# Two-block transformer kernel on one core: the passages between the expert blocks are reordered, and the dilated values' product is computed inside the block of queries and keys

## Chip, core and metric

The kernel runs on one core of one Trainium2 chip. Engines are named as in the profile: PE (TensorE matmul) and PEld (its weight loads), DVE (VectorE), ACT (ScalarE), POOL (GpSimd), SP (SyncE, here an issuer of DMAs). Times are device microseconds of one execution; the metric is the median of the runs.

## What is computed

Two transformer layers over 512 tokens of width 1024, all in float32. Both end in a PEER layer of experts, and these two hold most of the time:

```python
def peer_ffn(h, w_query, sub_keys, expert_u, expert_v):
    ...
        q = (xc @ w_query).reshape(PEER_CHUNK, PEER_HEADS, 2, PEER_HALF)
        s1 = jnp.einsum('thc,hnc->thn', q[:, :, 0], sub_keys[:, 0]).astype(jnp.float32)
        s2 = jnp.einsum('thc,hnc->thn', q[:, :, 1], sub_keys[:, 1]).astype(jnp.float32)
        v1, i1 = lax.top_k(s1, PEER_TOPK)
        v2, i2 = lax.top_k(s2, PEER_TOPK)
        cand = (v1[..., :, None] + v2[..., None, :]).reshape(PEER_CHUNK, PEER_HEADS, PEER_TOPK * PEER_TOPK)
        top, ci = lax.top_k(cand, PEER_TOPK)
        ...
        gate = jax.nn.softmax(top, axis=-1)
        act = jax.nn.gelu(jnp.einsum('td,thkd->thk', xc, u).astype(jnp.float32), approximate=False)
        wts = (gate * act).astype(xc.dtype)
        return jnp.einsum('thk,thkd->td', wts, vv)
```

There are 16384 experts of width 1024, 8 heads, and 16 experts chosen per head. The second layer also has an attention over strided keys (dilated), whose queries, keys and values are columns of one projection:

```python
    qa, ka, va, qb, kb, vb, gl = jnp.split(proj, IN_SPLITS, axis=-1)
    qa = rope(rms_norm(qa.reshape(b, s, DIL_HEADS, HEAD_DIM), qn_a), positions)
    ka = rope(rms_norm(ka.reshape(b, s, DIL_HEADS, HEAD_DIM), kn_a), positions)
    va = va.reshape(b, s, DIL_HEADS, HEAD_DIM)
```

## The kernel before

The program is a row of blocks. In a block every engine has its own list of instructions and they meet only by semaphores; at its end all engines wait for each other (in the trace: POOLq and PEq L83), so what one engine has left over at the end holds up all. Each float32 product is made of three passes of rounded halves: ACT rounds an operand (`hi`, a CAST), DVE subtracts (`lo`, TENSOR_TENSOR), and PE multiplies hi*hi, lo*hi and hi*lo. `rehearse` is ten small matmuls with no result of use at the start of some blocks.

**The expert layers** (`peer`, tags p1 and p2). For 384 of the 512 tokens every expert is computed densely, expert tile by expert tile: 128 tiles of 128 experts. For the first 128 tokens the chosen rows are gathered one by one (`Fetched`): POOL issues an indirect DMA per row into a ring of four, and DVE takes it (L1334 a dot product, L1342 an addition). Three blocks share the dense work:

- `peer_choose` (L1490). PE makes the scores of four token tiles of 128 tokens, DVE picks the best from them, and meanwhile the first 56 expert tiles (`TT * EARLY`, 14 per token tile) are multiplied by `A.multiply` (L1439, 24 matmuls into one of two banks). ACT empties a bank by `A.gelu` (L1421), then rounds the tile four further on (`split_hi`, L1410; four slabs) and stores the result (L1398). DVE's `split_lo` (L1429) stands between its steps of choosing, at places written out by hand. SP loads the tiles (L1389), four ahead. After the seventh tile of each token tile ACT waits for DVE's `shifted` and makes the exponential (L1568). `turn` (L1530) transposes the chosen indices and gates of a token tile, ACT copies them to `rows` (L1557).
- `peer_gates` (L1747 and on). PE multiplies the other 72 expert tiles and, behind each, one or two of 96 *steps*: a step is four tokens, whose one-hot rows `hot1` (times the gate) and `hot2` DVE makes (L1760, L1762) and whose remainder ACT makes (L1797), multiplied at L1787 into a ring of four. ACT copies the product to `kept` (L1815). Twelve *pieces* of eight steps each arise so; `kept` has room for two, so SP stores ten of them to `gates` in HBM (L1824), 2 MB each, and ACT waits for the store of piece n-2 before it writes piece n. SP's store of a piece stands two loads after its end. At the block's start ACT rounds all gates at once and DVE makes the relative rest of them (`rest_of_gates`, L1739 to L1745).
- `peer_values` (L1931): 128 tiles again, gates times activations times values.

**The second layer's projection.** `queries_keys` (L2996) multiplies nine chunks of 512 columns, seven of queries and keys and two of values (of the other attention); each has eight slabs, five of which are held split. Then `product` with tag va multiplies the dilated values, a chunk of 256 columns and one of 512, in a block of its own with its own split of the same input `hT`; `dilated_attention` (tag dat) follows.

## Time and profile before

| | us |
|---|---|
| median of three runs (3761.3 to 3764.9) | 3764.0 |
| the profiled execution, its own time | 3765.4 |
| its span, first to last instruction | 3763.2 |
| PE busy in it | 3601.9 |
| DVE busy | 2971.0 |
| ACT busy | 1724.5 |
| mean granted clock of PE, as a share of 2.4 GHz | 0.981 |

Where the first expert layer lies in the span: its choosing block from 667 to 926 us, the gates block to 1320, the values block to 1846; queries and keys run from 1870 to 2081, the dilated values to 2120; the second expert layer repeats the first one's blocks from 2573 on. The profile gives each instruction's start and length. Matmuls overlap: the next one starts before the one before is over, so distances from start to start count, and the number in square brackets behind a row is the time for which the engine idled before it, with what ended that. A clock below 1 (PEclk) is the share of full speed that PE was granted.

### The profile page before, as it was taken

The page shows a single profiled execution, that of the slowest core. Times are in us where ns is not written, and L with a number is a line of the kernel's source. Part 1 is how long each engine was busy: PE and PEld are TensorE (multiplying, and loading weights), DVE is VectorE, ACT ScalarE, POOL GpSimd, SP SyncE. Part 2 cuts the span into 40 slices and gives each one's busy share as a digit, 9 for nine tenths or more (in the row PEclk, how much of TensorE's full clock was granted, in tenths as well). Part 3 has the DMA queues.
Part 4 walks back from the last instruction along what each step waited for, and adds up shares of the span by engine and source line. Part 5 has one row for each costly group of instructions (what it writes and reads, how often), then busy time and mean ns, then how long its engine had stood idle before and what let it go on. Part 6 is the DMA issues. An engine that isn't in the chain of part 4 may idle for free. (4 is left out here: it accounts for less than half of the span.)

```text
span 3763.2 us, 54696 instructions
## 1 busy us (share of the span) xinstructions
PE 3601.9 (96%) x19490; PEld 3154.1 (84%) x19490; DVE 2971.0 (79%) x6556; ACT 1724.5 (46%) x3277; POOL 742.0 (20%) x523
## 2 busy tenths in 40 slices
PE   8868999999999999999899989999999999999999
PEld 7546788899999988888788757788999999888887
DVE  4674653898988799999677486446998888899998
ACT  4424443333666643333444464343345666433333
POOL 0000000000333344544100000000003333354442
PEclk9979999999999999999999999999999999999999
DMA  4352323455999899999522103323458999899997
GB/s 150 137 173 84 107 68 101 129 167 175 310 309 309 293 367 403 404 403 400 198 85 84 51 1 107 99 70 121 164 170 273 311 310 312 320 405 404 400 403 293
DMA packets 371886, 853.47 MB, mean 227 GB/s; under 512 B 35728, under 2 KB 184848, under 8 KB 368912
## 3 DMA queue, kind: packets, MB, share of 16 engines
q1 hardware_dynamic: 258912, 530.84, 39.9%
q0 software_dynamic: 73728, 268.47, 18.9%
q10 hardware_dynamic: 38976, 50.68, 4.0%
q8 instruction: 156, 2.56, 0.3%
q14 instruction: 114, 0.93, 0.1%
HBM read 753.26 MB, written 95.42 MB: 226 GB/s over the span
## 5 line engine op out<-in xcount | busy, mean ns | idle before, releaser
L1319 POOL DMA_INDIRECT p2f_row<-in_expert_u_rows,p2f_index x128 | 174.3, 1362 | 1306.5 <-POOLq L83 1019.1
L1319 POOL DMA_INDIRECT p1f_row<-in_peer_u_rows,p1f_index x128 | 175.0, 1367 | 963.9 <-POOLq L83 686.6
L1931 PE MATMUL p1v_out<-p1a_u_hi,p1v_w_hi 128*128 128x512 f32 x768 | 299.1, 390 | 0.0
L1931 PE MATMUL p1v_out<-p1a_u_lo,p1v_w_hi 128*128 128x512 f32 x768 | 299.0, 389 | 0.0
L1931 PE MATMUL p2v_out<-p2a_u_hi,p2v_w_hi 128*128 128x512 f32 x768 | 298.9, 389 | 0.0
L1931 PE MATMUL p1v_out<-p1a_u_hi,p1v_w_lo 128*128 128x512 f32 x768 | 298.8, 389 | 0.0
L1931 PE MATMUL p2v_out<-p2a_u_hi,p2v_w_lo 128*128 128x512 f32 x768 | 298.8, 389 | 0.0
L1931 PE MATMUL p2v_out<-p2a_u_lo,p2v_w_hi 128*128 128x512 f32 x768 | 298.8, 389 | 0.0
L1319 POOL DMA_INDIRECT p1f_row<-in_peer_v,p1f_index x128 | 197.7, 1544 | 238.7 <-DVE p1f_sum L1342 217.4
L1319 POOL DMA_INDIRECT p2f_row<-in_expert_v,p2f_index x128 | 189.9, 1483 | 238.3 <-DVE p2f_sum L1342 218.6
L1894 ACT CAST p1a_u_hi<-p1a_u 128x1024 fp32r<-128x1024 f32 x128 | 135.1, 1055 | 202.9 <-PE p1v_out L1931 184.6
L1894 ACT CAST p2a_u_hi<-p2a_u 128x1024 fp32r<-128x1024 f32 x128 | 135.1, 1055 | 199.8 <-PE p2v_out L1931 186.8
L1439 PE MATMUL p2g_pre<-p_x_hi,p2a_u_hi 128*128 128x384 f32 x576 | 197.1, 342 | 3.8 <-DVE p2a_u_lo L1429 3.8
L1439 PE MATMUL p1g_pre<-p_x_hi,p1a_u_hi 128*128 128x384 f32 x576 | 197.1, 342 | 3.8 <-DVE p1a_u_lo L1429 3.8
L1439 PE MATMUL p2g_pre<-p_x_hi,p2a_u_lo 128*128 128x384 f32 x576 | 193.7, 336 | 0.0
L1439 PE MATMUL p1g_pre<-p_x_hi,p1a_u_lo 128*128 128x384 f32 x576 | 193.7, 336 | 0.0
L1439 PE MATMUL p1g_pre<-p_x_lo,p1a_u_hi 128*128 128x384 f32 x576 | 193.4, 336 | 0.0
L1439 PE MATMUL p2g_pre<-p_x_lo,p2a_u_hi 128*128 128x384 f32 x576 | 193.3, 336 | 0.0
L1342 DVE SCALAR_TENSOR_TENSOR p2f_sum<-p2f_row,p2f_weight,p2f_sum 128x1024 f32<-128x1024 f32 x127 | 162.5, 1280 | 12.7 <-DMA p2f_row<-in_expert_v,p2f_index 11.7
L1342 DVE SCALAR_TENSOR_TENSOR p1f_sum<-p1f_row,p1f_weight,p1f_sum 128x1024 f32<-128x1024 f32 x127 | 162.5, 1279 | 11.0 <-DMA p1f_row<-in_peer_v,p1f_index 9.1
L1931 PEld LDWEIGHTS p1v_out<-p1a_u_hi,p1v_w_hi 128*128 128x128 f32 x768 | 144.3, 188 | 30.1
L1931 PEld LDWEIGHTS p1v_out<-p1a_u_hi,p1v_w_lo 128*128 128x128 f32 x768 | 144.3, 188 | 29.9
(740 smaller groups left out, 10804.0 us busy)
## 6 DMA issues: line engine op xcount, KB each, us to landing
p1a_u<-in_peer_u SPq DMA_DIRECT2D x128, 512.0 KB
p1a_u<-in_peer_v SPq DMA_DIRECT2D x128, 512.0 KB
p2a_u<-in_expert_u SPq DMA_DIRECT2D x128, 512.0 KB
p2a_u<-in_expert_v SPq DMA_DIRECT2D x128, 512.0 KB
gates<-p_kept SPq DMA_DIRECT2D x20, 2048.0 KB, 12.1
acts<-p1a_a ACTq DMA_DIRECT2D x128, 192.0 KB
p1w_a<-acts SPq DMA_DIRECT2D x128, 192.0 KB
acts<-p2a_a ACTq DMA_DIRECT2D x128, 192.0 KB
```

Of the source, the lines that this page charges most:

```text
L1319: self.nc.gpsimd.indirect_dma_start(self.row[:, n % self.RING, :], None, self.u_rows if dot else self.v_rows, bass.IndirectOffsetOnAxis(ap ...
L1342: V.scalar_tensor_tensor(self.sum[:], row, weight, self.sum[:], ALU.mult, ALU.add).then_inc(self.used, 1)
L1439: last = self.nc.tensor.matmul(self.pre[:, n % 2, 0:DENSE], u[:, s, k * P:(k + 1) * P], x[:, k, P:SEQ], start=(m == 0), stop=(m == 3 * DK ...
L1894: nc.scalar.copy(v_hi[:, n % VSLABS, :], v[:, n % LOADS, :]).then_inc(v_hi_ready, 1)
L1931: last = nc.tensor.matmul(out[:, o, :], lhs[:, s, t * P:(t + 1) * P], rhs[:, n % VSLABS, cols], start=(n == 0 and m == 0), stop=(n == KEYS ...
```

## The change

Five edits:

1. **Splits two tiles ahead, and a 57th tile in the choosing block.** DVE makes the splits of tiles 0 and 1 before anything else in `peer_choose`; each later split at the same place as before serves the tile two further on. The block multiplies 57 tiles (`INTO`) instead of 56; the gates block has 71 tiles, and its DVE list splits one tile further ahead than PE multiplies.
2. **The last token tile's turn moves to the gates block.** The chosen indices and gates live in `fetch.sum` now (`choice`), so that they outlast the block; PE transposes them after the first tile of the gates block, ACT copies them after its second gelu, and DVE waits for these copies (`rows_taken`) before its third tile.
3. **Gate rests per token tile.** The rounding and `rest_of_gates` are done for 128 columns at a time, at tiles 0, 16 and 40, in place of 384 at the start. No step stands behind the first tile; the 96 steps are spread over the 70 others.
4. **Pieces stored four tiles later.** SP stores a piece four tiles after the tile that completes it (`KEEP_AFTER`), and ACT and DVE split the first two value tiles at the end of the gates block instead of in the values block.
5. **Dilated values inside `queries_keys`.** The two chunks of the dilated values follow as tenth and eleventh chunk of that block, with its split input; ACT copies their results straight to `va`. To make room, `rot` and `prod` lie in `va`'s memory and the rope table in that of `masks`, which SP loads at the block's end, when all rotations are done.

The core of the diff:

```diff
 def peer_choose(...)
-            turn(pe, TT - 1)
+            A.multiply(pe, TT * EARLY)
...
-            take_rows(TT - 1)
+            A.gelu(act, TT * EARLY)
...
         @block.vector
         def _(dve):
             n = 0
+            for ahead in range(AHEAD):
+                A.split_lo(dve, ahead)
             for t in range(TT):
+                first_split = t * EARLY + AHEAD
                 dve.wait_ge(scored, t + 1)
...
-                A.split_lo(dve, t * EARLY)
+                A.split_lo(dve, first_split)
 def peer_gates(...)
...
-            return range(STEPS * i // LATE, STEPS * (i + 1) // LATE)
+            return range(ALL * max(i - 1, 0) // (TILES - 1), ALL * i // (TILES - 1))
...
+            ch = Chain(dve, step)
+            for i in range(TILES):
+                if i == 2:
+                    dve.wait_ge(rows_taken, 3)
+                if i in REST_AT:
+                    rest_of_gates(dve, ch, REST_AT.index(i))
+                if INTO + AHEAD - 1 + i < KEYS:
+                    A.split_lo(dve, INTO + AHEAD - 1 + i)
+                for s in steps_after(i):
...
+                for n in fetch.steps(i):
+                    fetch.take(dve, n)
+            for n in range(W.AHEAD):
+                W.split_lo(dve, n)
...
+            for i in range(TILES):
+                A.multiply(pe, INTO + i)
+                if i == 0:
+                    turn_choice(nc, C, *choice, tp).then_inc(turned, 1)
...
+                for t in range(STORED):
+                    if i == min(done_after((t + 1) * STEPS) + KEEP_AFTER, TILES - 1):
+                        keep(t)
 def queries_keys(...)
-    ALL = NC_ + 2
+    chunks = [(w_qk[c], False, None) for c in range(NC_)]
+    chunks += [(w_v[n], False, None) for n in range(2)] + w_va
+    ALL = len(chunks)
...
+            sp.wait_ge(rotated, TT * NC_)
+            for n, (to, source) in enumerate(transfers):
+                sp.dma_start(to, source).then_inc(transferred, 16)
...
-            product(nc, "va", C, hT, DK, SEQ,
```

How it moves the instructions, at three places. First DVE's list at the start of `peer_choose` in the first expert layer (p1a_u_lo is a split, p1c_val the maxima over the scores), before:

```order
L362 COPY p1m_qT<-p1q_out 128x512 x2
L172 UNCONDITIONAL_BRANCH
L1571 UNCONDITIONAL_BRANCH
L1577 MAX p1c_val<-p1c_score 128x8 x16
L1429 TENSOR_TENSOR p1a_u_lo<-p1a_u,p1a_u_hi 128x1024
```

and after:

```order
L362 COPY p1m_qT<-p1q_out 128x512 x2
L172 UNCONDITIONAL_BRANCH
L1587 UNCONDITIONAL_BRANCH
L1431 TENSOR_TENSOR p1a_u_lo<-p1a_u,p1a_u_hi 128x1024 x2
L1596 MAX p1c_val<-p1c_score 128x8 x16
L1431 TENSOR_TENSOR p1a_u_lo<-p1a_u,p1a_u_hi 128x1024
```

Two splits now stand ahead of the maxima. Second, DVE's list from the end of that block into `peer_gates` (p1w_g holds the gates' upper part, floor and rest, p1g_hot the hot tiles, p1f_row a gathered row), before:

```order
L1694 TENSOR_TENSOR p1c_gate<-p1c_weight,p1c_rtotal 128x128
L1490 UNCONDITIONAL_BRANCH
L1747 UNCONDITIONAL_BRANCH
L1429 TENSOR_TENSOR p1a_u_lo<-p1a_u,p1a_u_hi 128x1024
L1739 CAST p1w_g<-p1g_hot 128x384
L1740 TENSOR_SCALAR p1w_g<-p1g_hot 128x384
L1741 TENSOR_TENSOR p1w_g<-p_gateT,p1g_hot 128x384
L1743 RECIPROCAL p1w_g<-p1w_g 128x384
L1745 TENSOR_TENSOR p1w_g<-p1w_g 128x384
L1760 TENSOR_SCALAR p1g_hot<-iota,p_firstT,p1w_g 128x128 x4
L1762 TENSOR_TENSOR p1g_hot<-iota,p_secondT 128x512
L1334 ISA p1f_row,p1f_dots<-p1f_row,p1f_x 128x1024
```

and after:

```order
L1762 TENSOR_SCALAR p1w_g<-p1w_g 128x128
L1763 TENSOR_TENSOR p1w_g<-p_gateT,p1w_g 128x128
L1765 RECIPROCAL p1w_g<-p1w_g 128x128
L1767 TENSOR_TENSOR p1w_g<-p1w_g 128x128
L1431 TENSOR_TENSOR p1a_u_lo<-p1a_u,p1a_u_hi 128x1024
L1336 ISA p1f_row,p1f_dots<-p1f_row,p1f_x 128x1024
L1336 ISA p1f_dots 128x1
L1431 TENSOR_TENSOR p1a_u_lo<-p1a_u,p1a_u_hi 128x1024
L1785 TENSOR_SCALAR p1g_hot<-iota,p_firstT,p1w_g 128x128 x4
L1787 TENSOR_TENSOR p1g_hot<-iota,p_secondT 128x512
```

The first gathered row and a second split stand now ahead of the first hot tile. Third, SP's list in the gates block (p1a_u loads of expert tiles, gates the stores of pieces), before:

```order
L1820 UNCONDITIONAL_BRANCH
L1389 DMA p1a_u<-in_peer_u 128x1024 x8
L1824 DMA gates<-p_kept 128x32x128
L1389 DMA p1a_u<-in_peer_u 128x1024 x6
L1824 DMA gates<-p_kept 128x32x128
```

and after:

```order
L1869 UNCONDITIONAL_BRANCH
L1391 DMA p1a_u<-in_peer_u 128x1024 x11
L1873 DMA gates<-p_kept 128x32x128
L1391 DMA p1a_u<-in_peer_u 128x1024 x6
L1873 DMA gates<-p_kept 128x32x128
```

The eight loads before were those of tiles 60 to 67, the eleven after are those of tiles 61 to 71: the first store stands four loads further back.

## Rows read from the trace of the kernel before

**Rows 1.** The page's part 1: busy time, share of span, instructions.
```profile
PE 3601.9 (96%) x19490; PEld 3154.1 (84%) x19490; DVE 2971.0 (79%) x6556; ACT 1724.5 (46%) x3277; POOL 742.0 (20%) x523
```

**Rows 2.** Windows: stretch, its length, then busy PE, PEld, DVE, ACT, POOL, PEclk.
```profile
675.40:704.40 29.00, 27.88 (x145) 27.00 (x146) 28.86 (x164) 7.14 (x10) 0.00 (x0) 0.92 0.48 154
831.90:877.80 45.90, 45.90 (x267) 45.88 (x267) 45.41 (x149) 17.17 (x23) 0.00 (x0) 1.00 0.47 156
```

**Rows 3.** Timeline, start of choosing, first layer: start, length, engine, line, operation, [idle before].
```profile
667.08 1.99 ACT L1410 CAST p1a_u_hi<-p1a_u 128x1024 fp32r<-128x1024 f32 x2 [1.70 <-PEq L83]
...
674.14 1.20 DVE L1429 TENSOR_TENSOR p1a_u_lo<-p1a_u,p1a_u_hi 128x1024 fp32r<-128x1024 f32 x1
...
675.39 0.69 PE L1439 MATMUL p1c_pre<-p_x_hi,p1a_u_hi 128*128 128x384 f32 x1 [4.48 <-DVE p1a_u_lo L1429]
...
695.96 0.45 PE L1439 MATMUL p1c_pre<-p_x_hi,p1a_u_hi 128*128 128x384 f32 x1 [0.86 <-DVE p1a_u_lo L1429]
```

**Rows 4.** Timeline, from choosing into the gates block, first layer.
```profile
923.91 0.38 PE L1530 MATMUL p1c_tp<-ident,p1c_chosen 128*128 128x128 f32 x2
...
924.50 1.04 ACT L1410 CAST p1a_u_hi<-p1a_u 128x1024 fp32r<-128x1024 f32 x1
...
926.90 0.51 ACT L1802 CAST p1g_hot<-p_gateT 128x384 fp32r<-128x384 f32 x1 [0.87 <-PEq L83]
926.93 1.23 DVE L1429 TENSOR_TENSOR p1a_u_lo<-p1a_u,p1a_u_hi 128x1024 fp32r<-128x1024 f32 x1 [9.55 <-PEq L83]
...
928.21 0.45 PE L1439 MATMUL p1g_pre<-p_x_hi,p1a_u_hi 128*128 128x384 f32 x1 [3.81 <-DVE p1a_u_lo L1429]
...
932.26 1.11 DVE L1760 TENSOR_SCALAR p1g_hot<-iota,p_firstT,p1w_g 128x128 fp32r<-128x128 f32 x4
...
933.28 0.68 DVE L1762 TENSOR_TENSOR p1g_hot<-iota,p_secondT 128x512 fp32r<-128x512 f32 x1
...
935.49 0.30 PE L1787 MATMUL p1g_prod<-p1g_hot 128*128 128x128 f32 x1 [1.27 <-ACT p_x_hi L1797]
```

**Rows 5.** Timeline of DVE and ACT about the last token tile's exponential, first layer.
```profile
892.66 0.27 DVE L1629 TENSOR_TENSOR p1c_shifted<-p1c_top 128x128 f32<-128x128 f32 x1
...
894.99 0.49 ACT L1421 ACTIVATE p1a_a<-p1c_pre 128x384 f32<-128x384 f32 x1 [2.73 <-PE p1c_pre L1439]
...
896.43 1.28 ACT L1568 ACT_TABLE_LOAD   x1
...
899.35 0.49 ACT L1421 ACTIVATE p1a_a<-p1c_pre 128x384 f32<-128x384 f32 x1
```

**Rows 6.** Waits of PE: who waited for whom, us in total, times, longest.
```profile
PE p2g_prod L1787 <- issue: 1.2, 1, 1.2
```

**Rows 7.** POOL's first gather; its queue's packets in 926.9 to 932.0 and to 933.4.
```profile
927.70 1.43 POOL L1319 DMA_INDIRECT p1f_row<-in_peer_u_rows,p1f_index  x1 [686.56 <-POOLq L83]
...
q0 software_dynamic: 103, 0.42, 21.5%
...
q0 software_dynamic: 213, 0.81, 38.4%
```

**Rows 8.** Waits of DVE in the gates block, first layer.
```profile
DVE p1g_hot L1760 <- PE p1g_prod L1787: 40.9, 52, 1.3
```

**Rows 9.** Stores of pieces: SP's timeline, the page's DMA issues, ACT's copy of piece 3.
```profile
965.01 0.38 SPq L1824 DMA_DIRECT2D gates<-p_kept  x1
966.90 24.28 SPq L1389 DMA_DIRECT2D p1a_u<-in_peer_u  x6
...
gates<-p_kept SPq DMA_DIRECT2D x20, 2048.0 KB, 12.1
...
1002.87 0.58 ACT L1815 COPY p_kept<-p1g_prod 128x512 f32<-128x512 f32 x1
```

**Rows 10.** Timeline of PE, from queries and keys to the dilated values.
```profile
2082.62 0.35 PE L127 MATMUL va_out<-ident 128*128 128x128 f32 x1 [1.60 <-PEq L83]
...
2085.39 0.36 PE L252 MATMUL va_out<-va_w_hi,va_x_hi 128*128 128x256 f32 x1 [0.30 <-ACT va_w_hi L310]
```

More of the change, by code:

```diff
@@ L1521, in _ @@
         def _(sp):
-            for n in range(A.LOADS, TT * EARLY + A.LOADS):
+            for n in range(A.LOADS, INTO + A.LOADS):
                 A.load(sp, n)
@@ L1699, in _, with peer_gates @@
                     n += 1
-def peer_gates(nc, tag, C, rows, gates, kept, A, W, fetch):
+def peer_gates(nc, tag, C, rows, choice, gates, kept, A, W, fetch):
     first, second, gate = rows
@@ L1742, in rest_of_gates, with done_after @@
+        def done_after(steps):
+            return next(i for i in range(TILES) if ALL * i // (TILES - 1) >= steps)
+        def rest_of_gates(dve, ch, n):
+            V, cols = nc.vector, slice(n * P, (n + 1) * P)
+            dve.wait_ge(top_made, n + 1)
+            ch.add(V.tensor_scalar(floor[:, cols], gate_top[:, cols], TINY, None, ALU.max))
+            ch.add(V.tensor_tensor(gate_rest[:, cols], gate[:, cols], gate_top[:, cols], ALU.subtract))
             ch.wait()
-            ch.add(V.reciprocal(floor, floor))
+            ch.add(V.reciprocal(floor[:, cols], floor[:, cols]))
@@ L2985, in _ @@
             rehearse(nc, C["ident"], out[:, 0, :])
-            for c in range(ALL):
+            for c, (src, stepped, _) in enumerate(chunks):
+                cols = src.shape[2]
                 for k in range(DK):
@@ L2995, in _ @@
                         for n, (xs, ws) in enumerate(((x_hi, w_hi), (x_lo, w_hi), (x_hi, w_lo))):
-                            last = nc.tensor.matmul(out[:, t, :], xs[:, k, t * P:(t + 1) * P], ws[:, s % SLABS, :],
+                            last = nc.tensor.matmul(out[:, t, 0:cols], xs[:, k, tile], ws[:, s % SLABS, 0:cols],
                                                     start=(k == 0 and n == 0), stop=(k == DK - 1 and n == 2),
```

283 lines of the change are left out of this document (150 added, 133 removed).

## Prediction, made before the changed kernel was run

> **What bounds the kernel now.** The page's busy line comes first: PE is busy for 3601.9 of 3763.2 us [rows 1], and the chain that ended last is PE alone. So nothing but a gap on PE, or a stretch in which PE's clock is at half, can be won or lost; DVE, ACT and the queues count only where PE waits for them. I therefore walked along PE's timeline and listed the places where the next matmul starts late. The change touches five such places: the start of the choosing block, the passage from there to the gates block, the first tiles of the gates block, the passage to the values block, and the passage from queries and keys to the dilated values. The first four occur twice, once per expert layer, with waits that agree within 0.1 us except where I say otherwise; I give those of the first layer. One "multiply" is the 24 matmuls of one expert tile: the undisturbed window of [rows 2] holds eleven in 45.9 us, so 4.17 us each.
>
> **Start of the choosing block.** Before, DVE does 16 maxima over the scores ahead of its first split, so the split starts at 674.14 although ACT had its half of tiles 0 and 1 ready by 669.1; PE starts at 675.39 after 4.48 us of idling (since 670.9, the end of its score matmuls), and idles 0.86 us more before its fifth tile [rows 3]. The half clock costs more: the window of the first six multiplies and that second gap takes 29.0 us at a granted clock of 0.92 [rows 2]; 6 x 4.17 = 25.0 and 0.9 of gap leave 3.0 us. In the changed order both splits (1.20 us each) stand ahead of the maxima, at 668.1 to 670.5, so the scores hide them. All later splits keep DVE's own pace but serve a tile two further on: before, DVE's third split stood where now the fifth stands, and PE has then 2 x 4.17 us more. The maxima are not delayed, since DVE waited for the scores anyway. I take the whole: 4.5 + 0.9 + 3.0 = **8.4 us**. If the clock fell all the same, 3.0 of it would stay away; I think not: there is no idling left there. It fell to its lower level (1.2 GHz) after 4.5 us of idling here and after 3.8 us at the gates seam [rows 3, 4].
>
> **A wait that takes part of it back.** PE then runs 8.4 us ahead of DVE's choosing, whose length is DVE's own (it is busy for 28.86 of 29.0 and 45.41 of 45.9 us in the two windows [rows 2], and has 56 splits and four token tiles of choosing whatever PE does). ACT, after the seventh multiply of each token tile, waits for "shifted" from DVE before the exponential, and queued behind it on ACT is the gelu of the eighth tile, which PE needs before its tenth (two banks). In the last token tile the difference is ready at 892.66 + 0.27 = 892.9, and from the table load at 896.43 to the next gelu at 899.35 it is 2.9 us [rows 5]. Before, the gelu of the seventh came at 894.99, later than that, so nobody waited. Now it would come at 886.6; the next gelu ends at 892.9 + 2.9 + 0.5 = 896.3, and PE wants the bank at 894.8 - 8.4 + 8.3 = 894.7: **1.6 us lost**. In the other three token tiles the same sum comes out 0 to 1 us short of a wait. Bounds 0 and 4.
> Those 2.9 us hold two switches of ACT's table and the exponential, so a switch is at most 1.5 us [rows 5]. The Trainium skill ("ScalarE: Activation LUTs", What ACT_TABLE_LOAD costs) gives about 2.66 us for every switch, with a drain. By that figure the two would take 5.3 us, and this wait would be 1.6 + 2.7 = 4.3 us, and the token tile before it would wait about 2 us too; the trace does not agree with it here, and its number decides.
>
> **Choosing to gates.** Before: PE is through with choosing at 923.91; then come three transposes (0.24), ACT's gelu and its split from 924.50 (0.93 until the next instruction can start), three copies until 926.03, the change of block, DVE's split of 1.23 us at 926.93, and PE starts at 928.21: 4.3 us [rows 4]. Now the copies and the split are gone from between, but ACT's gelu and split of the 57th tile still stand there (PE's end + 1.6), and the change of block takes 0.87, ACT's idle before 926.90: 2.5 us, and the transposes come later (0.25). Gain 4.3 - 2.75 = **1.55 us**.
>
> **First tiles of the gates block.** Before, 7.3 us pass from PE's first matmul (928.21) to its first gates step (935.49), where 4.17 would do: 3.1 us, of which 1.27 is the wait for ACT's products and 1.8 half clock [rows 4]; later waits add about 0.5 in the first layer and 1.5 in the second, the largest 1.2 [rows 6]. Now the reciprocal is a third as long, but I expect no gain here, since another wait takes its place: DVE has now a row of the gathered table to take *ahead* of the first hot tile. Let G be the start of the block (926.9 in the old trace). GpSimd issues the first gather at G + 0.8; of its 128 packets 103 have started by G + 5.1, and 213 by G + 6.5 [rows 7]; I take G + 5.8. DVE: dot product until 7.0, split until 8.1, hot tiles (932.26 to 933.96: 1.7 us [rows 4]) until 9.8; ACT and the semaphores 1.5 more (933.96 to 935.49): 11.3. PE: two multiplies and the transposes, ready at 8.6, so it waits **2.7**. Then DVE waits for `rows_taken`: ACT makes the products (until 11.2), gelu and split (12.5), three copies (13.0); queued behind that wait on DVE are the next split, hot tiles and rows. Split until 14.2, hot tiles 16.0, ACT 17.5; PE is there at 12.2 + 4.2 = 16.4: **1.1 more**. Third step: none. 3.8 in all, bounds 3.0 and 4.6 from the two packet counts. After such idling the clock may fall again (before: 1.8 us of the 3.1); while PE waits for DVE most of that is hidden, I take 0.6. So 4.4 now against 3.6 and 4.6 before: **0.8 lost** in the first layer, 0.2 won in the second (I expect the 1.2 to go, since the stores are moved away from the loads). After that DVE gains on PE, as before, when it waited 40.9 us for PE in the block [rows 8].
>
> **Costed at nothing.** Gates to values: the two value splits are now done early, but PE's rehearsal matmuls fill the time, and the weights w cannot be made before the block; the second tile's split was never late. Two casts more on ACT at the end of the gates block stand beside a multiply of 4.17 us. The gates' two further roundings on ACT and chains on DVE lie in its 40.9 us of waiting; without that cover some 2 us. The stores, see the last rival.
>
> **Queries and keys to dilated values.** PE idles 1.60 us at the change of block, then rehearses and waits from 2082.62 until the first matmul of the values at 2085.39 [rows 10]: 4.4 us. Now the ring of five split slabs runs on over the chunk's end, and the next matmul follows at the usual distance, which is 0.1 us less than the profile's length of one: **4.5 us**. The 192 matmuls stay. All four results of a chunk are now copied by ACT alone; the last one is as late as before within 0.1 us. The masks' load stands behind all slab loads on SP, as it did.
>
> **The sum.** First layer 8.4 - 1.6 + 1.55 - 0.8 = 7.55; second 8.4 - 1.6 + 1.55 + 0.2 = 8.55; values 4.5: 20.6 us. The profiled run took 3765.4 us, span 3763.2, the median of the runs is 3764.0; I subtract from the median: **3743.5 us**.
>
> **Rivals.**
> *More comes back as waits* (0.17). DVE's choosing and its splits two tiles further on lean on ACT's halves, which come only after PE has freed a slab; if ACT's wait for "shifted" costs its upper bound in each layer, the clock falls at the start of the block after all, and the gates start costs 4.6: 2 x (2.4 + 1.5 + 0.8) = 9.4 less, **3753 us**. For it: DVE has almost no slack in that block. Against: in the first token tile, where it was late before, each split has now 1 to 4 us to spare in my count, later more.
> *Less comes back* (0.15). The gathered row lands early and the clock stays up: the gates start then costs about 1.5 instead of 4.4, ACT's wait is 0: 2 x 4.5 = 9 more, **3734.5 us**. For it: in the old trace DVE is at work during all of the gather's start, now it is idle.
> Beside it stands the Trainium skill's "SBUF — State Buffer" (the "DVE blocks DMA" trap): some DVE operations keep GpSimd from writing its descriptors. If that made the 3 us from issue to first packet, this rival would be the likelier; no row shows the cause.
> *No difference* (0.04): PE's wins turn into waits at the next block, because DVE's work ends when it did. Against: DVE waited 9.55 us for the next block [rows 4], of which the change of block is one; 6 us of slack are more than the split of the 57th tile needs.
> *Slower* (0.06). The piece stores. The first was issued at 965.01; it now stands behind the load of tile 71, the fourth of the six that began at 966.90 and ran over 24 us, so at about 981, and takes 12.1 us to land: 993. ACT may write the third piece into that room at 1002.87 [rows 9], so 10 us are left. If the stores are later or slower by more than those 10 us, ACT stops at each piece from the third on, and behind it the gelus and PE: each further us costs 10 x 2 layers = 20 us; at 2 us beyond the margin 3764 - 21 + 40 = **3783 us**. Against: the loads hurry rather than wait in the new order.
>
> **Chances.** Forecast 0.58 (3739 to 3748 by its bounds), the others as given. The range reaches over most of the two neighbours: 3735 to 3753. A measurement of this kernel can tell about 0.2% (7.5 us) from no change: faster 0.90, within it 0.05, slower 0.05.
>
> **What would show it.** Right: the first expert matmul directly after the scores, no half clock there; a seam of about 2.5 us; then PE waiting 2 to 3 us at the first gates step and 1 at the second; no gap at 2081. Wrong: PE waiting on u_lo within the choosing block, ACT waiting on stores (`kept`), or an unchanged clock dip at the start.

## The result, and the profile after it

The changed kernel takes **3741.8 us** in the median of five runs (3739.1 to 3743.0), the kernel before 3761.3 on the same chip (five runs, 3760.4 to 3764.9): 0.9945 of it, with a 95% interval of 0.9932 to 0.9958, so 19.5 us by the medians and 20.7 by the ratio. A second set on another occasion gave 3741.5, 0.9946 (0.9932 to 0.996). The forecast was 3743.5, a gain of 20.6 from the 3764.0 of the runs before. The total came out right partly by luck: one term was missing (a loss of 4.5 us at the passage from gates to values), and the gains of other steps were taken too small by about as much.

The profiled execution has a span of 3740.0 us, 23.2 less than before. The busy line of its page, to be set beside [rows 1]:

```profile
PE 3586.7 (96%) x19470; PEld 3146.0 (84%) x19470; DVE 2966.7 (79%) x6558; ACT 1713.2 (46%) x3277; POOL 676.8 (18%) x523
```

PE still sets the time. Where the 23.2 us went is read by dividing both traces at PE's first and last matmul of each block (start to start, worked out from the timelines). One expert tile, 4.17 us, has moved from the gates to the choosing block, and the table takes it off again:

| stretch of PE | before | after | gain | gain that was forecast |
|---|---|---|---|---|
| ahead of the first layer's scores | 667.1 | 665.8 | 1.3 | untouched |
| scores to first multiply, each layer | 8.29 | 3.57 | 4.7 and 4.7 | } 6.8 and 6.8 |
| choosing block, after less one tile | 248.3, 248.4 | 245.3, 245.3 | 3.0 and 3.1 | } |
| choosing to gates, less the transposes' 0.24 before | 4.2, 4.2 | 2.8, 2.8 | 1.4 and 1.4 | 1.55 and 1.55 |
| gates block, before less one tile, transposes 0.24 off after | 386.5, 387.5 | 386.4, 386.7 | 0.1 and 0.9 | -0.8 and 0.2 |
| gates to values | 1.70, 1.67 | 3.40, 4.45 | **-1.7 and -2.8** | 0 and 0 |
| values block | 525.95, 526.01 | 525.99, 526.37 | 0 and -0.4 | untouched |
| queries and keys to attention | 255.3 | 250.4 | 4.9 | 4.5 |
| everything else | | | 2.6 | untouched |

The places that the change touches hold 19.3 of the 23.2. The rest comes from stages whose code is the same; their stretches of half clock differ from one execution to the next (6.8 us long before and 3.4 after in two stages between 2400 and 2500, for example).

**Start of the choosing block.** The first group is the timeline of DVE and PE, beside [rows 3]; the second is the window of the first six multiplies, beside the first row of [rows 2].

```profile
666.87 2.36 DVE L1431 TENSOR_TENSOR p1a_u_lo<-p1a_u,p1a_u_hi 128x1024 fp32r<-128x1024 f32 x2 [1.99 <-ACT p1a_u_hi L1412]
...
665.82 3.81 PE L1555 MATMUL p1c_score<-p1f_row,p1m_qT 128*128 128x128 f32 x32 [1.67 <-PEq L83]
669.38 0.42 PE L1441 MATMUL p1c_pre<-p_x_hi,p1a_u_hi 128*128 128x384 f32 x1
```
```profile
669.38:694.46 25.08, 25.08 (x148) 25.08 (x147) 24.72 (x133) 8.72 (x12) 0.00 (x0) 1.00 0.49 164
```

Both splits run under the scores, the first multiply follows the scores without idling, and six multiplies take 25.1 us at a granted clock of 1.00, where they took 29.0 at 0.92.

**The exponential of the last token tile.** PE's one gap in the choosing block, and ACT's timeline around it (beside [rows 5]):

```profile
892.91 0.34 PE L1441 MATMUL p1c_pre<-p_x_hi,p1a_u_lo 128*128 128x384 f32 x1
893.99 0.41 PE L1441 MATMUL p1c_pre<-p_x_hi,p1a_u_hi 128*128 128x384 f32 x1 [0.74 <-ACT p1a_a L1423]
```
```profile
886.41 1.28 ACT L1584 ACT_TABLE_LOAD   x1
891.73 0.31 ACT L1584 ACTIVATE p1c_weight<-p1c_shifted 128x128 f32<-128x128 f32 x1 [4.04 <-DVE p1c_shifted L1648]
892.06 1.28 ACT L1423 ACT_TABLE_LOAD   x1
893.35 0.49 ACT L1423 ACTIVATE p1a_a<-p1c_pre 128x384 f32<-128x384 f32 x1
```

ACT loads the exponential's table at 886.41, ahead of its wait. Behind the wait come only the exponential, one load of 1.28 us and the gelu: 2.1 us, where the forecast had 3.4 (2.9 and the gelu's 0.5).

**Choosing to gates, and the first gates step.** PE, then DVE; beside [rows 4].

```profile
918.85 0.34 PE L1441 MATMUL p1c_pre<-p_x_hi,p1a_u_lo 128*128 128x384 f32 x1
921.69 0.41 PE L1441 MATMUL p1g_pre<-p_x_hi,p1a_u_hi 128*128 128x384 f32 x1 [2.50 <-PEq L83]
...
933.12 0.30 PE L1815 MATMUL p1g_prod<-p1g_hot 128*128 128x128 f32 x1 [2.49 <-ACT p_x_hi L1832]
```
```profile
923.50 1.22 DVE L1431 TENSOR_TENSOR p1a_u_lo<-p1a_u,p1a_u_hi 128x1024 fp32r<-128x1024 f32 x1
927.66 1.23 DVE L1336 CUSTOM_DVE_ANT_0 p1f_row<-p1f_row,p1f_x 128x1024 f32<-128x1024 f32 x1 [2.94 <-DMA p1f_row<-in_peer_u_rows,p1f_index]
928.82 0.08 DVE L1336 DVE_READ_ACCUMULATOR2_ANT p1f_dots<- 128x1 f32 x1
928.82 1.22 DVE L1431 TENSOR_TENSOR p1a_u_lo<-p1a_u,p1a_u_hi 128x1024 fp32r<-128x1024 f32 x1
```

DVE idles 2.94 us for the first gathered row with split and hot tile queued behind it, as foretold, and PE waits 2.49 us at the first step. In the second layer it is 1.4 us (PE comes later there, since its clock is at half at the block's start), and the wait of 1.2 us that stood in [rows 6] is not there any more. All waits of PE in the second layer's gates block:

```profile
PE p2g_pre L1441 <- PEq L83: 2.5, 1, 2.5
PE p2g_prod L1815 <- ACT p_x_hi L1832: 1.4, 1, 1.4
```

**Gates to values.** Here is the loss. PE's last step and its first rehearsal matmul, in both layers:

```profile
1308.35 0.28 PE L1815 MATMUL p1g_prod<-p_x_lo,p1g_hot 128*128 128x128 f32 x1
1311.76 0.46 PE L127 MATMUL p1v_out<-ident 128*128 128x128 f32 x2 [3.13 <-PEq L83]
```
```profile
3201.78 0.28 PE L1815 MATMUL p2g_prod<-p_x_lo,p2g_hot 128*128 128x128 f32 x1
3206.23 0.55 PE L127 MATMUL p2v_out<-ident 128*128 128x128 f32 x1 [4.18 <-PEq L83]
```

Before, PE idled 1.4 us at this place. The other engines' last work in the first layer's gates block, in the timeline:

```profile
1299.52 1.29 DVE L1344 SCALAR_TENSOR_TENSOR p1f_sum<-p1f_row,p1f_weight,p1f_sum 128x1024 f32<-128x1024 f32 x1
1304.31 1.23 DVE L1489 TENSOR_TENSOR p1a_u_lo<-p1a_u,p1a_u_hi 128x1024 fp32r<-128x1024 f32 x1 [3.51 <-ACT p1a_u_hi L1485]
1307.60 1.23 DVE L1489 TENSOR_TENSOR p1a_u_lo<-p1a_u,p1a_u_hi 128x1024 fp32r<-128x1024 f32 x1 [2.06 <-ACT p1a_u_hi L1485]
```
```profile
1301.92 0.94 POOL L1321 DMA_INDIRECT p1f_row<-in_peer_v,p1f_index  x1 [0.30 <-issue]
```
```profile
1308.35 1.07 ACT L1860 COPY p_kept<-p1g_prod 128x512 f32<-128x512 f32 x2 [0.40 <-ACT p1a_a L1423]
```

ACT is the last of PE, DVE and ACT to be through, at 1309.4, and PE starts 2.3 us later; before, it was 0.8 us. Two things are new at the end of the block: the value casts and splits, and the distance of the last gathered row from the end. In the trace's records, GpSimd's last gather is issued at 1301.92, the last packet of the gathers' queue ends at 1307.15, and GpSimd's final drain (the last instruction of its list, begun at 1300.85) ends at 1310.99; in the second layer 3195.35, 3201.39 and 3205.47. "Landed" means the end of that last packet in what follows. That made two theories for the loss, and most of the experiments are about them.

### The profile page after: what moved, and what is told of

It is laid out like the page before. It is cut to its first block and busy times, and to the rows that moved or that the text cites. A ratio compares the mean times of both kernels' runs of the same rounds, so it can differ in the third digit from the quotient of the medians.

```text
span 3740.0 us, 54632 instructions
## 1 busy us (share of the span) xinstructions
PE 3586.7 (96%) x19470; PEld 3146.0 (84%) x19470; DVE 2966.7 (79%) x6558; ACT 1713.2 (46%) x3277; POOL 676.8 (18%) x523
## 3 DMA queue, kind: packets, MB, share of 16 engines
q0 software_dynamic: 73728, 268.47, 19.3%
## 5 line engine op out<-in xcount | busy, mean ns | idle before, releaser
L1321 POOL DMA_INDIRECT p2f_row<-in_expert_v,p2f_index x128 | 167.9, 1312 | 257.7 <-DVE p2f_sum L1344 228.8
L1321 POOL DMA_INDIRECT p1f_row<-in_peer_v,p1f_index x128 | 166.9, 1304 | 255.4 <-DVE p1f_sum L1344 226.5
L1489 DVE TENSOR_TENSOR p2a_u_lo<-p2a_u,p2a_u_hi 128x1024 fp32r<-128x1024 f32 x128 | 156.5, 1222 | 32.0 <-ACT p2a_u_hi L1485 31.6
L1489 DVE TENSOR_TENSOR p1a_u_lo<-p1a_u,p1a_u_hi 128x1024 fp32r<-128x1024 f32 x128 | 156.4, 1222 | 30.7 <-ACT p1a_u_hi L1485 30.5
L1431 DVE TENSOR_TENSOR p2a_u_lo<-p2a_u,p2a_u_hi 128x1024 fp32r<-128x1024 f32 x128 | 156.3, 1222 | 27.6 <-ACT p2a_u_hi L1412 24.8
L1431 DVE TENSOR_TENSOR p1a_u_lo<-p1a_u,p1a_u_hi 128x1024 fp32r<-128x1024 f32 x128 | 156.3, 1222 | 26.9 <-ACT p1a_u_hi L1412 24.8
## 6 DMA issues: line engine op xcount, KB each, us to landing
gates<-p_kept SPq DMA_DIRECT2D x20, 2048.0 KB, 15.3
```

Of the source, the lines that this page charges most:

```text
L1321: self.nc.gpsimd.indirect_dma_start(self.row[:, n % self.RING, :], None, self.u_rows if dot else self.v_rows, bass.IndirectOffsetOnAxis(ap ...
L1431: self.nc.vector.tensor_tensor(self.u_lo[:, s, :], self.u[:, n % self.LOADS, :], self.u_hi[:, s, :], ALU.subtract).then_inc(self.u_ready, 1)
L1489: self.nc.vector.tensor_tensor(self.v_lo[:, n % self.slabs, :], self.v[:, n % self.LOADS, :], self.v_hi[:, n % self.slabs, :], ALU.subtrac ...
```

## The experiments

Each run was made beside runs of the kernel before; medians and the ratio to it are given, and a difference to the changed kernel is against 3741.8 (3741.5 in the set with the last three runs). The kernel before took 3761.2 to 3761.8 us in all four sets (the result's and three of experiments), so that they can be set side by side. Single medians scatter by 1 to 2 us, and the length of half clock in untouched stages differs from one execution to the next. So for the small effects the lengths of the stretches in the profiled executions decide.

### The dilated values inside, alone

The kernel before with this part of the diff only (`queries_keys` and `block2`).

```
-            queries_keys(nc, C, hT, A["w_qk_2"], A["w_vb_2"], cosg, sing, qkT, raw)
+        queries_keys(nc, C, hT, A["w_qk_2"], A["w_vb_2"], w_va, cosg, sing, qkT, raw, va[:].rearrange("p t n -> p (t n)"),
+                     [(masks[:], A["masks"])])
...
-            product(nc, "va", C, hT, DK, SEQ,
```

> The kernel before with one part of the change alone: the dilated values computed inside the block of queries and keys. By the forecast's step the passage of 4.4 us (1.60 of idling, rehearsal and wait until 2085.39) goes and nothing comes in its place: 3761.3 - 4.5 = 3757 us, with no gap on PE between the last chunk of the queries and keys and the values. In the trace of the whole change that stage lasts 245.3 us against 250.05, which says 4.8. Rival: the copies, now on ACT alone, and the slabs of another width make PE wait inside the block, and the gain measured there is only a clock that happened to be up: then 3760 or more.

Measured 3758.3 us, ratio 0.9992 (0.9983 to 1.0001). The passage is gone: PE goes from its first `qk` matmul to the first of the attention in 248.9 us against 255.3 before and 250.4 in the changed kernel, with no gap between the last chunk of queries and keys and the values. At the start of this stage the clock is at half for 17.0 us in both the kernel before and the changed one, and for 13.6 us here, which is the 1.5 us between 248.9 and 250.4. With the clock alike, the part is worth 4.9 us. The medians show 3.2, and the interval reaches from -0.4 to 6.4, so that the medians alone would not prove a gain. In the profiled execution the second layer's gates block was 396.6 us long against 391.7 before, which hid the rest, and PE's waits in it name the reason:

```profile
PE p2g_prod L1787 <- issue: 2.9, 2, 2.3
```

The larger of the two (2.3 us) is the wait that [rows 6] show with 1.2, in the same tile. It is of another size each time, and here the clock was at half for 6.8 us behind it.

### The splits made after the maxima again

```
-            for ahead in range(AHEAD):
-                A.split_lo(dve, ahead)
             for t in range(TT):
...
                 n += HALVES
+                if t == 0:
+                    for ahead in range(AHEAD):
+                        A.split_lo(dve, ahead)
                 A.split_lo(dve, first_split)
```

> The changed kernel, but in the first token tile DVE makes its two splits ahead after the 16 maxima, where the first split stood before. Theory one, as forecast: idling and clock count both. PE again waits 4.5 us behind its scores, its clock falls (3.0 us), and of these 7.5 us the 0.9 us for which PE now waits behind ACT's exponential in the last token tile comes back: 6.6 us in each layer, 3742 + 13 = 3755 us, with a granted clock at half for 6 to 7 us near 673 and near 2570. Rival: only the idling counts, because what PE loses at the start it wins back later (DVE's choosing sets the block's length, as it is busy for all of it): then the block ends where it did, and the time is within 3 us of 3742.

Measured 3751.0 us, ratio 0.9972 (0.9962 to 0.9983): 9.2 more. Here are DVE's rows at the start, then the window of 25.1 us from the first multiply on:

```profile
669.92 3.27 DVE L1594 MAX8 p1c_val<-p1c_score 128x8 f32<-128x128 f32 x16 [4.79 <-PE p1c_score L1555]
673.10 3.48 DVE L1431 TENSOR_TENSOR p1a_u_lo<-p1a_u,p1a_u_hi 128x1024 fp32r<-128x1024 f32 x3
```
```profile
674.36:699.44 25.08, 25.07 (x135) 25.08 (x136) 24.97 (x133) 7.14 (x10) 0.00 (x0) 0.93 0.50 168
```

The passage from scores to first multiply is 8.29 us again, with 4.48 of idling, and the clock is at 0.93. From scores to the block's end it takes 5.3 and 6.0 us more than in the changed kernel. Idling is 4.7 of that; the clock's fall costs 1.6 and 2.3 against the version with no fall and no wait (below); the wait at the exponential is gone and gives 1.0 back. So the theory's sign and mechanism hold, and the rival (the block ends when DVE does, whatever PE lost) falls. The theory's size, 13 us, was too high: the clock's share is 1.6 to 2.3 us a layer here, where [rows 2] gave 3.0.

### Why the passage to the values grew: rows ended early

```
-            first, per, tiles, n = 0, FETCHED_IN_GATES, late, tile
+            first, per, tiles, n = 0, FETCHED_IN_GATES, late - 2, tile
...
-        return range(first + per * n // tiles, first + per * min(n + 1, tiles) // tiles)
+        return range(first + per * min(n, tiles) // tiles, first + per * min(n + 1, tiles) // tiles)
```

> The changed kernel, but the 80 gathered rows of the gates block are spread over its first 69 tiles instead of all 71, so DVE takes none in the last two. It asks why PE idles 3.1 and 4.2 us at the passage from gates to values, 1.7 and 2.8 more than before, which the forecast had put at nothing. Theory: GpSimd's last gather is issued 1.5 us after DVE has used the row two slots ahead of it, lands 5 to 7 us later, and GpSimd leaves the block 3.5 us behind that, at 1311.0 and 3205.5, while all other engines are through by 1309.5 and 3202.9. With the rows taken two tiles earlier GpSimd is through first; PE idles 1.4 us again, and the half clock after it may be shorter: 1.6 + 2.7 = 4.3 us less, up to 7 with the clock, 3735 to 3737.5 us. Rival: the two casts and the two splits of values at the block's end make it long; then the idling stays 3.1 and 4.2 us and the time 3742.

Measured 3739.0 us, ratio 0.994 (0.9926 to 0.9953). PE at the passage in the first layer:

```profile
1309.12 0.28 PE L1815 MATMUL p1g_prod<-p_x_lo,p1g_hot 128*128 128x128 f32 x1
1310.99 0.46 PE L127 MATMUL p1v_out<-ident 128*128 128x128 f32 x2 [1.59 <-PEq L83]
```

It is 1.87 us from matmul to matmul here and 1.86 in the second layer, where the changed kernel has 3.40 and 4.45. The casts and splits of the values are all in place. That is 4.1 us, in the profiled execution also a shorter values block (524.4 us against 526.0 and 526.4, with the clock up at its start). The median moved by 2.8, less than the 4.3 to 7 forecast, and medians scatter by 1 to 2 us. GpSimd's drain ends at 1300.84 here, long before all others are through.

### The value splits back in their block

```
-    LOADS, G, AHEAD = 4, EGROUP, 2
+    LOADS, G, AHEAD = 4, EGROUP, 0
```

> The changed kernel, but all value splits are made in the values block again, as before the change. Same question as in the run with the rows ended early, from the other side. Theory (GpSimd's last gather ends the block): the idling of 3.1 and 4.2 us stays, the first values matmul follows the rehearsal as before, 3742 to 3743 us. Rival (ACT's casts and DVE's splits at the end of the gates block): idling back to 1.4 us in both layers, 3738 us or less.

Measured 3743.6 us, ratio 0.9952 (0.9938 to 0.9966). The passage stays long without the casts and splits (3.64 and 3.67 us), and the row that names the wait reads:

```profile
PE p1v_out L127 <- PEq L83: 3.4, 1, 3.4
```

The rival falls. No gain of the values' early splits can be seen either: the values blocks are 526.7 and 527.1 us long without them, and 525.8 to 527.2 in the two traces of the changed kernel.

### The rows taken later

```
+                if i == TILES - 1:
+                    for n in range(W.AHEAD):
+                        W.split_lo(dve, n)
                 for n in fetch.steps(i):
                     fetch.take(dve, n)
-            for n in range(W.AHEAD):
-                W.split_lo(dve, n)
```

> The changed kernel, but in the last tile of the gates block DVE takes the two gathered rows after its two value splits instead of before them. It measures how firmly the last gather holds the block. In the traces so far GpSimd left the block 3.8 to 4.1 us after the last gathered row had landed, and the row landed 6.3 to 7.2 us after DVE had used the one whose place it takes. Theory: DVE's use ends at the second value split, 1308.8, + 2.5 = 1311.3, so 10.5 us later than now; each of the two passages grows by that, to 14 us in place of 3.4 and 4.5: 3742 + 20 = 3762 us, plus up to 3 for the clock. Rival (the gather doesn't hold the block; values' splits or drains do): 3742 to 3746.

Measured 3760.6 us, ratio 0.9997 (0.9987 to 1.0006): 19.1 more than the changed kernel, from moving two rows' instructions, 1.2 and 1.3 us long, on an engine that is idle at that place. The forecast was 3762. PE's passages are 13.4 us long in both layers. The chain stands in three rows, of DVE, GpSimd and PE:

```profile
1310.79 1.28 DVE L1344 SCALAR_TENSOR_TENSOR p1f_sum<-p1f_row,p1f_weight,p1f_sum 128x1024 f32<-128x1024 f32 x1
```
```profile
1313.18 0.94 POOL L1321 DMA_INDIRECT p1f_row<-in_peer_v,p1f_index  x1 [0.30 <-issue]
```
```profile
1309.25 0.28 PE L1816 MATMUL p1g_prod<-p_x_lo,p1g_hot 128*128 128x128 f32 x1
1322.64 0.77 PE L127 MATMUL p1v_out<-ident 128*128 128x128 f32 x2 [13.12 <-PEq L83]
```

DVE's last use ends at 1312.07, the gather is issued at 1313.18 and has landed at 1318.04, GpSimd's drain ends at 1321.87, and PE starts at 1322.64: 10.6 us behind DVE's use. In the changed kernel the same chain is 1300.81 to 1311.76, 10.9 us, and 12.0 us in the second layer. PE's idling is this chain less the distance from DVE's last use to PE's end. That distance was 11.3 us before (1307.90 to 1319.2), and is 7.8 in the changed kernel in both layers: 10.9 - 7.8 = 3.1, 12.0 - 7.8 = 4.2, as the two rows above have it.

The rows taken earlier, unmoved and later agree: the last gathered row holds the block wherever its chain ends last.

### No gathered row in the first tile

```
-            first, per, tiles, n = 0, FETCHED_IN_GATES, late, tile
+            first, per, tiles, n = 0, FETCHED_IN_GATES, late - 1, tile - 1
```

> The changed kernel, but DVE takes no gathered row in the first tile of the gates block (the 80 rows are spread over the other 70 tiles). Theory, as forecast: PE waits at its first gates step for the hot tile, DVE makes it after the split, and both stand behind the first gathered row, which DVE reads at 927.66 after 2.94 us of idling. Without the row DVE makes the second split as soon as ACT's half is there, at about 924.8, and the hot tile by 927.6; ACT's products are ready at 929, before PE has done its two multiplies and the transposes at 930.3: the wait of 2.5 us at the first step and 1.4 us in the second layer goes, 2 to 2.5 us of it net in the first layer and 1.4 in the second; with less half clock 3737 to 3739 us. Rival: the idling moves on, since the three copies of the last token tile and the wait for them stand right behind: then one wait of 1 to 2 us at the second step takes its place and the time is 3740 to 3742.

Measured 3740.3 us, ratio 0.9936 (0.9923 to 0.995). PE's wait at the first step is gone, and DVE and PE show what took its place:

```profile
925.70 1.12 DVE L1785 TENSOR_SCALAR p1g_hot<-iota,p_firstT,p1w_g 128x128 fp32r<-128x128 f32 x4
...
933.31 1.22 DVE L1431 TENSOR_TENSOR p1a_u_lo<-p1a_u,p1a_u_hi 128x1024 fp32r<-128x1024 f32 x1 [4.34 <-ACT p_gateT L1848]
```
```profile
PE p1g_prod L1815 <- ACT p_x_hi L1832: 2.0, 1, 2.0
```

DVE makes the hot tile at 925.70 instead of 929.95 but then waits 4.34 us for the three copies of the last token tile, and PE waits 2.0 us at the second step. The rival had the mechanism. The gates blocks still are 2.1 and 1.7 us shorter (384.5 and 385.2); most of that is one stretch of half clock less in each layer (3.4 us at half, 1.7 us of time), and the waits themselves are only 0.5 and 0.1 us shorter. By the median the run can't be told from the changed kernel.

### The exponential one tile later

```
-                    if i == 6:
+                    if i == 7:
                         act.wait_ge(shifted_ready, t + 1)
```

> The changed kernel, but ACT waits for the difference and makes its exponential after the gelu of the eighth multiply of a token tile instead of the seventh. Theory, as forecast in kind: PE's gap of 0.74 and 0.76 us at 892.9 and 2786.1 comes from the gelu queued behind that wait and goes; nothing comes in its place in this block, since DVE needs the exponential only after its fourteenth split: 3742 - 1.5 = 3740.5 us. Rival: the two switches of ACT's table, 2.9 us with the exponential, now stand before the gelu of the ninth tile with the same effect one tile on, and the gap moves: 3742.

Measured 3739.5 us, ratio 0.9938 (0.9925 to 0.9952). The choosing blocks are 248.46 and 248.47 us long against 249.47 in both layers of the changed kernel, and PE has no gap in them. So this wait cost 1.0 us per layer: more than the 0.74 of idling. From start to start the two matmuls around the gap are 1.08 us apart where 0.17 is usual, so 0.9 of it lies right there. The rival (the gap moves one tile on) falls.

### The stores two tiles later instead of four

```
-    GATE_TILES, REST_AT, KEEP_AFTER = DENSE // P, (0, 16, 40), 4
+    GATE_TILES, REST_AT, KEEP_AFTER = DENSE // P, (0, 16, 40), 2
```

> The changed kernel, but the pieces of the gates are stored two tiles after they are made instead of four. It tells whether moving the stores won anything: the forecast gave 0 in all and expected the wait of 1.2 us in the second layer to go with the move. Theory: the stores collide with the loads that DVE's splits wait for; back at two tiles PE has a wait of 0.7 us in the first and 1.2 to 1.4 us in the second layer again, 3743.5 us. Rival: those waits went because DVE and ACT run further ahead at the start of the block, and the place of the stores makes no difference: 3742.

Measured 3743.3 us, ratio 0.9948 (0.9934 to 0.9962). By the medians this can't be told from the changed kernel. By the trace, waits of the old kind are back, though not in the old tile. In the second layer PE waits at one step, and ACT's row just before shows for what:

```profile
PE p2g_prod L1815 <- issue: 1.3, 1, 1.3
```
```profile
2911.78 1.05 ACT L1412 CAST p2a_u_hi<-p2a_u 128x1024 fp32r<-128x1024 f32 x1 [2.90 <-DMA p2a_u<-in_expert_u]
```

ACT's rounding of an expert tile waited 2.90 us for the tile's load, 17 us after the issue of a store; DVE's split, its hot tile and PE's step stand behind it. The wait of [rows 6] in the kernel before has the same row ahead of it:

```profile
2890.88 1.05 ACT L1410 CAST p2a_u_hi<-p2a_u 128x1024 fp32r<-128x1024 f32 x1 [3.39 <-DMA p2a_u<-in_expert_u]
```

In the first layer PE has one such wait, of 0.53 us. Of the 20 gates blocks read with the stores four tiles later none has a wait of PE beyond its second step; of the six with two tiles (here, before, and before with the values inside) all have at least one. Behind a store, ACT waits for an expert tile's load (over 0.2 us, ending 14 to 19 us after the store's issue) four to eight times in each of these six blocks, and once in all the 20 others together (0.7 us). So the place of the stores takes the waits of [rows 6] away. Its worth is known only roughly: the waits of PE are 1.8 us in all here, and the gates blocks (387.4 and 387.6 us) are 0.7 longer in each layer than in the first trace of the changed kernel, but such blocks differ by 1.4 us among themselves.

### A version with three waits mended, and one more

No gathered row in the first tile and the last two, the wait for the three copies moved down, the exponential one tile later:

```
-            first, per, tiles, n = 0, FETCHED_IN_GATES, late, tile
+            first, per, tiles, n = 0, FETCHED_IN_GATES, late - 3, tile - 1
...
-                    if i == 6:
+                    if i == 7:
...
-                if i == 2:
+                if i == 8:
                     dve.wait_ge(rows_taken, 3)
```

> A version that should beat both kernels: the changed kernel with no gathered row in the first tile and none in the last two, the wait for the three copies of the last token tile moved from the third to the ninth tile of the gates block, and ACT's exponential one tile later. If the causes are as I hold them, each gain stands: 4.3 us at the passage to the values, 3.5 to 4.5 at the first gates steps, 1.5 at the exponential, and some half clock less: 3742 - 9 to 12 = 3730 to 3733 us. If the waits only change places it is 3738 or more.

Measured **3728.7 us**, ratio 0.9907 (0.9892 to 0.9922), 13.1 under the changed kernel and 1.3 under the range forecast. Stretch by stretch: choosing 1.0 in each layer, gates 2.9 and 3.0 (383.78 and 383.90), gates to values 1.5 and 2.6: 12.0. PE's waits in the first layer from the gates block's start on are two:

```profile
PE p1g_pre L1441 <- PEq L83: 2.5, 1, 2.5
PE p1v_out L127 <- PEq L83: 1.6, 1, 1.6
```

The first of them is the passage from choosing to gates, and the next version goes at it. The two banks for `pre` are kept over both blocks, and ACT's gelu of the 57th tile is made in the second:

```
+            A.place(phase_tools(nc, shared, tag + "s")[1])
             peer_choose(nc, tag + "c", C, qT, keys, rows, choice, A, fetch)
...
-            A.gelu(act, TT * EARLY)
...
             round_gates(act, 0)
+            A.gelu(act, INTO - 1)
```

> The mended version of the run before (3728.7 us), with one step more: ACT's gelu and split of the 57th tile, which follow PE's last multiply of the choosing block by 1.6 us and keep all engines in it, are made as the first work of the gates block. Theory: the passage from choosing to gates, 2.84 us from matmul to matmul, is made of this gelu and split and the change of block, so it shrinks by 1 to 1.4 us to about 1.6; with the clock's fall at the block's start (3.4 us at half) gone too, another 1.7: 2 to 6 us less, 3723 to 3727. Rival: the 0.87 us of the change and a drain of ACT that it ends with are what counts, and the passage shrinks by less than 0.5 us: 3728.

Measured **3723.4 us**, ratio 0.9895 (0.9879 to 0.9911), 5.3 under the version before it and 37.8 under the kernel before (3761.2 in this set). PE at the passage:

```profile
920.36 0.34 PE L1444 MATMUL p1s_pre<-p_x_hi,p1a_u_lo 128*128 128x384 f32 x1
921.75 0.41 PE L1444 MATMUL p1s_pre<-p_x_hi,p1a_u_hi 128*128 128x384 f32 x1 [1.06 <-PEq L83]
```

It is 1.40 us from matmul to matmul instead of 2.84, the clock doesn't fall behind it in either layer (it did in both in the version before), and no other wait appears in the gates block. 2 x 1.44 and 2 x 1.7 of half clock would be 6.3; 5.3 were measured.

The changed kernel itself, run once more beside the last two:

> The changed kernel once more, unaltered, beside the two that follow. 3741.8 us within 3. Its last gathered row of the gates block again ends it: an idling of PE of 3 to 4 us at both passages to the values.

It took 3741.5 us; PE's passages to the values were 3.68 and 3.59 us long. Its first gates steps waited 1.0 and 0.6 us, where the first trace has 2.5 and 1.4, and its second ones 0.7 in both layers, where the first trace has no such wait. In the eight profiled executions that have DVE's row in the first tile, two layers each, this wait is 2.4 to 2.7 us in the four layers where the clock stayed up at the block's start, and 0.6 to 1.4 in the twelve where it was at half then. The gates block as a whole varies less: 385.5 to 386.9 us with the stores at their new place.

## Why the prediction was right, and where it wasn't

**Start of choosing, right in mechanism, in size within 1 us.** Forecast 8.4 less 1.6, measured 7.8 in both layers, and 8.8 without the 1.0 that the exponential's wait took back. Every part of the 8.4 is seen: no idling of 4.5, no second gap, a clock of 1.00. Undoing the order alone brought 5.3 and 6.0 back, in which the exponential's wait of 1.0 has gone: 6.3 and 7.0 of the 8.8. The remaining 1.8 to 2.5 are the second gap, which does not come back in that run, where the later splits still serve a tile two further on, and part of the clock's fall.

**The exponential, right place, cost too high.** Forecast 1.6, measured 1.0 (the run with the exponential later). The step that failed is the 2.9 us put behind the wait: they hold two loads of ACT's table, one of which stands ahead of ACT's wait when ACT is early, so that only one is behind it. A load is 1.28 us in the trace, and the gelu starts 1.29 us after its load did. The Trainium skill ("ScalarE: Activation LUTs", What ACT_TABLE_LOAD costs) gives about 2.66 us for a switch, of which about 1.28 are the load and 1.38 a drain. The load agrees with the trace; the drain isn't seen, and by the full 2.66 the wait would have been larger than forecast, where it was smaller.

**Choosing to gates.** Forecast 2.5 of idling, measured 2.50. Which part of it was what is shown by the last version: gelu and split are 1.4, the change of block 1.06.

**First gates tiles, the sum nearly right, its parts not, and the kernel before counted too low.** The last version's gates blocks have neither a wait nor half clock and take 382.4 and 382.3 us. Against these the changed kernel's blocks in the first trace, 386.7 and 386.9, lose 4.2 and 4.6; forecast 2.7 + 1.1 + 0.6 = 4.4. But the waits are 2.5 and 1.4 and not 3.8, and the rest is half clock, one stretch of 3.4 us in the first layer and two in the second, where 0.6 was taken. Reckoned in the same way (a tile of 4.17 off, 0.24 for the transposes added) the blocks before lose 4.3 and 5.5, where the forecast had 3.6 and 4.6. Hence 0.1 and 0.9 won instead of 0.8 lost and 0.2 won.

The first wait came as forecast where the clock was up: DVE's dot product starts 6.15 us after the block's start (ACT's first instruction, 921.51) instead of 5.8, PE is ready at 9.1 instead of 8.6, and 2.5 instead of 2.7 lie between. Where the clock is at half from the start, PE comes later and the wait is 0.6 to 1.4. The second wait was 0.7, not 1.1, where there was one. The mended version, which has half clock at the start of both blocks, is 2.9 and 3.0 us shorter than the first trace there, and 2.1 and 1.6 shorter than the second. The 1.2 of [rows 6] went, as said, and the run with the stores two tiles later shows that it went because of the stores' place.

**Gates to values, wrong.** "Costed at nothing: gates to values" is the step that failed. I asked who makes what PE needs next, and not who leaves the block last. The change spreads 96 steps over 70 tiles in place of eight over each six; the step whose ring slot DVE's last hot tile needs runs two tiles before the end instead of three (DVE begins that hot tile at 1296.75, 11.9 us ahead of PE's end; before, at 1303.85, 15.3 us ahead), and behind that hot tile DVE takes the last two rows. That much I read from the two orders of instructions, and no run tries it alone. What the runs show is what follows: a row taken by DVE keeps PE from the next block for another 10.6 to 12.0 us, and with 7.8 left PE idles. It cost 1.7 and 2.8 us, 4.5 in all, in the first trace; the second trace of the same kernel has passages of 3.7 and 3.6 us, so 3.9 in all. The old trace could have told: GpSimd's drain ended at 1318.2 there, 1.6 us before the barrier let go for the others' sake, so this chain had 1.6 us of slack and lost 3.5 of its distance.

**Queries and keys to values, right.** Forecast 4.5, measured 4.9.

**The stores.** Forecast 0 with a rival at 3783. The rival's margin was larger than reckoned: the first store was issued at 968.2, not 981, and it had landed at 984.9, nearly 16 us before ACT's third piece at 1000.7; the longest of all stores took 17.5 us to land. No wait on a store is in the trace. The step "forecast 0" was too low: the better place takes away PE's waits for late loads, about 1.4 to 1.8 us.

**The sum.** 20.6 forecast; the choosing block and its wait gave 1.9 more, the first gates tiles 1.5 more, the passage from queries and keys 0.4 more, the passage to gates 0.3 less, the passage to values 4.5 less and the start of the values 0.4 less: 19.2, against 19.3 in the table, 19.5 by the medians and 20.7 by the ratio. The number was closer than its terms, and that is luck: a loss of 4.5 that nobody had counted met 3.8 of gains taken too small.

## What to carry to other kernels

At the end of a block, ask of every engine when it leaves it, not only of those that make something for the next: an engine that waits out its last transfer is one of them. Here 9.5 to 10.6 us had to lie between the last row taken and PE's end (the chain of 10.9 to 12.0 less the 1.4 for which PE idles anyway). Waits at a passage stand in a row, so removing the first one alone (the row in the first tile) moved the median by 1.5 us, no more than medians scatter, while all together gave 13.1, where 9 to 12 had been forecast; count until no wait is left. And a load of ACT's table that stands ahead of the wait is hidden in it: look on which side of the wait it stands before it is counted.

## What the hardware showed beyond that

- GpSimd's drain at the end of a block ends 3.8 to 4.1 us after the last packet of the last row that it gathered, in all 26 passages read (13 executions, two layers). Where it is the last, PE starts 0.8 us behind. That last packet itself ends 4.8 to 7.4 us after the gather's issue.
- Of 20 passages from choosing to gates with 2.5 us of idling, the granted clock was at half (1.2 GHz) right at the gates block's start in 15 and stayed at 2.4 GHz in 5, all five in the first layer; in four of these five it fell behind the next idling, of 2.4 to 2.7 us, at the first step. After the 1.06 us of the last version it did not fall in either layer.
- A load of ACT's table takes 1.28 us, for the exponential as for the gelu, and the exponential's load began at 886.41, while ACT still waited for the input until 891.73.
- With each store of 2 MB issued two tiles after its piece, ACT waited for expert tiles 14 to 19 us behind the issue, up to 3.4 us at a time before the change and 2.9 in the run that put the stores back; with the stores issued four tiles after their piece such a wait is missing in 19 of 20 blocks.
